# Where the operands of a matmul lie: down products, gate and up rows, and the load of the constants

## The chip, the cores and the metric

One Trainium2 chip, one core. The metric is the device time of one launch of the whole kernel, in microseconds. The kernel before takes 5654.88 us (median of three runs, 5647.37 to 5656.9).

## The reference

Two transformer blocks on 1024 tokens of width 1024, all in float32. The first holds an RWKV branch and a sparse attention branch. The second has two layers: latent attention beside a gated linear recurrence, then a SwiGLU feed-forward, dense in layer 0 and routed to 2 of 8 experts in layer 1. The parts that matter here:

```python
def _swiglu(h, w_gate, w_up, w_down):
    return (jax.nn.silu(h @ w_gate) * (h @ w_up)) @ w_down
...
    xs = xf[tok_sorted]
    hid = jax.nn.silu(lax.ragged_dot(xs, w_gate, group_sizes)) * lax.ragged_dot(xs, w_up, group_sizes)
    ys = lax.ragged_dot(hid, w_down, group_sizes)
```

The dense feed-forward is 1024 x 2816 x 1024, each expert's 1024 x 3584 x 1024.

## The kernel before

The program is a row of stages. Each has its own block of instructions for the five engines and ends in a barrier of all of them. `first_block` runs first. Its first stage, `norm_in` (`norm_transpose`), loads the eight row blocks of x, norms them (ScalarE squares, VectorE scales) and transposes them on TensorE, with the identity matrix `eye`, the first 128 columns of the constants `cst`. Ahead of it stands a stage of its own, `load_constants`, in which SyncE loads `cst` (128 x 3808) and `vec` (128 x 107) and waits for both.

The feed-forwards are `swiglu_passes` (dense, tiles named `dense_*`) and `expert_passes` (tiles named `experts_*`). Every float32 product is made of three matmuls of type float32r: each operand is split into a rounded part `high` and a rest `low`, and high x high, high x low and low x high are summed in PSUM. Both run over chunks of 128 hidden units; a chunk's weights are one load of 1.5 MB (`raw`: gate, up, down, each 128 x 1024), which ScalarE rounds to `high` and VectorE subtracts to `low`.

- Gate and up products: the stationary operand is a 128 x 128 block k of the weights, the moving operand is block k of the transposed rows `xs_high` or `xs_low` (`dense_xs_parts` in the dense block), 256 or 288 columns wide. Three matmuls for each k, 8 blocks, two products: 48 matmuls for each chunk.
- Down products: the stationary operand is 128 columns of the hidden values, `hid_high` or `hid_low`, the moving operand is a half, 512 columns, of the chunk's down weights. 12 matmuls for each chunk at 256 slots, 16 at 288.

The experts run 8 passes of 28 chunks, four of 288 slots and four of 256 as the trace's counts say (112 chunks of each width); the dense block runs 4 passes of 22 chunks with 256 rows.

```python
last = nc.tensor.matmul(ps[:, m, 0:width], w[:, u, m, c], x[:, k, 0:width], ...)        # gate, up: L3237
last = nc.tensor.matmul(ps[:, 2 + 2 * a + h, :], x, w[:, v, 2, c], ...)                 # down: L3229
```

(The second argument is the stationary operand, the third the moving one. In the rows of a profile the moving operand is named first.) Weights are prepared two chunks ahead: ScalarE and VectorE work on chunk n+2 while TensorE works on chunk n, and SyncE asks for a load when `split` says that the buffer `raw` is free.

Tiles lie in SBUF one behind the other, in the order in which the stage names them (`st.sb`). A tile's address here is its byte offset in each partition, and its *rest* is that address modulo 512. Blocks of 128 float32 columns are 512 bytes, so all 128-column blocks of a tile whose rows are whole multiples of 512 bytes have the tile's rest. `xs_high` of the experts has rows of 288 columns, 1152 bytes, so that its block k lies 128 k bytes further modulo 512. The float32r products of the other stages (`proj`, L2099; `out_proj`, L1725 to L1727) have both operands at the same rest, 448.

Of the kernel before, what the change touches and what calls it, by code (L numbers as in the profile page):

```python
# [8 lines left out]
F32R = mybir.dt.float32r  # L9
# [8 lines left out]
P = 128  # L18
NT = T // P
KD = D // P  # L20
# [122 lines left out]

def load_constants(core):
    nc, d = core.nc, core.dram
    st = Stage(core, "const")
    loaded = st.sem("loaded")
    with nc.Block("const") as block:
        @block.sync
        def _(sp):  # L150
            sp.dma_start(core.cst[:, :], d["constants"]).then_inc(loaded, 16)
            sp.dma_start(core.vec[:, :], d["vectors"]).then_inc(loaded, 16)
            sp.wait_ge(loaded, 32)
    st.end()


def norm_transpose(core, name, x, xT, gain, source, out=None, room=None, router=None, moves=()):

# [5 lines left out]
    U = 4 if router is None else 3  # L164
    router_in, beside = st.sem("router_in"), st.sem("beside")
    parts = xT if isinstance(xT, tuple) else None
# [10 lines left out]
    with nc.Block(name) as block:  # L177
        @block.sync
        def _(sp):
            if router is not None:  # L180
                sp.dma_start(router[:, :, :], core.dram["router"]).then_inc(router_in, 16)
            for b in range(NT):
                sp.dma_start(x[:, b, :], source[b * P:(b + 1) * P, :]).then_inc(loaded[b], 16)
                if b == 0:
                    sp.dma_start(row[:, :], core.dram[gain].to_broadcast([P, D])).then_inc(gain_in, 16)
            for to, origin in moves:
                sp.dma_start(to, origin).then_inc(beside, 16)
# [70 lines left out]
        def _(pe):  # L258
            def score(b):
# [3 lines left out]
                for k in range(KD):  # L263
                    nc.tensor.matmul(core.ps[:, 6, b * NEXP:(b + 1) * NEXP], xT[:, k, b * P:(b + 1) * P], router[:, k, :],
                                     start=(k == 0), stop=(k == KD - 1))

            for b in range(NT):
                pe.wait_ge(scaled, b + 1)
                if b >= U:
                    pe.wait_ge(rounded, b - U + 1)  # L270
                    if parts:
                        pe.wait_ge(placed, b - U + 1)
                for k in range(KD):
                    last = nc.tensor.transpose(ps4[:, b % U, k, :], xs[:, b % R, k * P:(k + 1) * P], core.c("eye"))
                last.then_inc(turned, 1)
                if router is not None and b:
                    score(b - 1)
# [2452 lines left out]
def swiglu_passes(core, name, NC, weights, out, experts=None, tiles=None, residual=None):  # L2730
# [19 lines left out]
    high = st.sb("high", [P, NB, 3, D], F32R)  # L2750
    low = st.sb("low", [P, NB, 3, D], F32R)
    index = st.sb("index", [P, 2], U32)
    xs = st.sb("xs", [P, 2, D])
# [4 lines left out]
    hid = st.sb("hid", [P, 2, SLOTS])  # L2758
    hid_high = st.sb("hid_high", [P, 2, SLOTS], F32R)
    hid_low = st.sb("hid_low", [P, 2, SLOTS], F32R)  # L2760
    y = st.sb("y", [P, 2, D])
# [311 lines left out]
def expert_passes(core, name, NC, weights, out, experts, tiles, slots, index):  # L3073
# [17 lines left out]
    high = st.sb("high", [P, NB, 3, D], F32R)  # L3091
    low = st.sb("low", [P, NB, 3, D], F32R)
    token = st.sb("token", [P, NT], U32)
    xs = st.sb("xs", [P, 3, D])
    xs_high = st.sb("xs_high", [P, KD, ROOM], F32R)
    xs_low = st.sb("xs_low", [P, KD, ROOM], F32R)
    silu = st.sb("silu", [P, 2, ROOM])
    hid = st.sb("hid", [P, 2, ROOM])


    hid_high = st.sb("hid_high", [P, 2, KEPT], F32R)
    hid_low = st.sb("hid_low", [P, 2, MAIN], F32R)
    y = st.sb("y", [P, 3, D])
# [385 lines left out]
def build(nc, dram, dump=None, until=None):  # L3489

    with ExitStack() as ctx:
        core = Core(nc, dram, ctx)
        load_constants(core)
        first_block(core, dump)
# [84 lines left out]
def first_block(core, dump):  # L3579
    nc, d = core.nc, core.dram  # L3580
    with nc.sbuf_tensor("big", [P, 5, 4, T], F32) as big:
        flat = big[:, :, :, :].rearrange("p a j n -> p (a j) n")
        with nc.sbuf_tensor("masks", [P, offset(NT) - offset(TOPK // P)], F32) as masks, nc.sbuf_tensor("small", [P, T], F32) as small:
            down, queries, relu = flat[:, 0:4, :], flat[:, 8:10, :], flat[:, 10:12, :]
            with nc.sbuf_tensor("index_weight", [P, NT, IDX_HEADS], F32) as weight, ExitStack() as s2:
                xT = split_tensors(core, s2, "xT", [P, KD, T])
                norm_transpose(core, "norm_in", as_rows(flat[:, 0:8, :]), xT, "norm_row", d["x"])
                projections(core, "proj", d["w_in"], xT, [(4, ACT.Copy, lambda n: at(down, n), None),
# [202 lines left out]
```

## Time and profile before

| what | value |
|---|---|
| median of 3 runs | 5654.88 us |
| the profiled execution | 5654.06 us, span of its instructions 5652.3 us |
| granted TensorE clock, mean | 0.954 |
| TensorE busy | 92% of the span |
| VectorE, ScalarE busy | 49%, 39% |
| experts (gate, up, down) | 3415.6 to 5581 us |
| dense block | 1860 to 2611 us |

The duration that a row gives for a matmul includes its way through the array, which overlaps with the next matmul. The rate is read from the starts: the distance of two starts divided by the number of matmuls between them.

### The profile page before, as it was taken

How to read it: one execution, taken by the hardware profiler on the slowest of the kernel's cores; microseconds unless marked ns; L12 is line 12 of the kernel's file. 1: busy time of each engine (PE TensorE's matmuls, PEld its weight loads, DVE VectorE, ACT ScalarE, POOL GpSimd, SP SyncE). 2: the span in 40 equal slices, each digit the busy share in tenths (PEclk: the TensorE clock that was granted, in tenths of full speed). 3: DMA queues.
4: the chain of work that ended last, by engine and by line, in shares of the span. 5: the costliest groups of instructions: out<-in, count | busy, mean ns of one | idle time of the engine just before them, and what ended most of it. 6: DMA issues, size and time to landing. Idle time of an engine off the chain costs nothing. (4 is left out here: it accounts for less than half of the span.)

```text
span 5652.3 us, 97257 instructions
## 1 busy us (share of the span) xinstructions
PE 5191.5 (92%) x38308; PEld 4533.0 (80%) x38309; DVE 2744.8 (49%) x4394; ACT 2225.0 (39%) x3437; POOL 345.9 (6%) x564
## 2 busy tenths in 40 slices
PE   6896989899899899997989988999999999999994
PEld 5574977677677899996877677989898999999994
DVE  2497545333844455554156444444444555555444
ACT  2353236232443444443234423333334444444432
POOL 0121100000600000000023001000000000000001
PEclk8996999999999999998999998999999999999997
DMA  1110010311003655553100424444444554555544
GB/s 68 49 64 22 0 36 1 120 59 34 3 17 120 238 211 203 190 205 115 45 16 19 137 112 174 155 162 155 159 154 170 187 188 179 204 187 188 184 156 187
DMA packets 104464, 688.49 MB, mean 122 GB/s; under 512 B 12304, under 2 KB 16160, under 8 KB 63136
## 3 DMA queue, kind: packets, MB, share of 16 engines
q1 hardware_dynamic: 90608, 639.74, 31.4%
q0 software_dynamic: 8816, 27.44, 1.3%
q10 hardware_dynamic: 4800, 17.83, 0.8%
q8 instruction: 186, 3.05, 0.2%
q14 instruction: 54, 0.44, 0.0%
HBM read 622.67 MB, written 62.29 MB: 121 GB/s over the span
## 5 line engine op out<-in xcount | busy, mean ns | idle before, releaser
L3373 DVE TENSOR_TENSOR experts_low<-experts_raw,experts_high 128x1024 fp32r<-128x1024 f32 x678 | 810.8, 1224 | 1005.9 <-ACT experts_high L3302 1005.9
L3237 PE MATMUL ps<-experts_xs_high,experts_high 128*128 128x256 f32 (+1 forms) x3584 | 1038.4, 290 | 38.0 <-issue 36.1
L3237 PE MATMUL ps<-experts_xs_high,experts_low 128*128 128x256 f32 (+1 forms) x3584 | 1039.2, 290 | 2.0 <-issue 1.9
L3237 PE MATMUL ps<-experts_xs_low,experts_high 128*128 128x256 f32 (+1 forms) x3584 | 1037.8, 290 | 0.0
L3237 PEld LDWEIGHTS ps<-experts_xs_high,experts_high 128*128 128x128 f32 x3584 | 681.4, 190 | 53.2 <-issue 43.7
L3302 ACT ACTIVATE experts_high<-experts_raw 128x1024 fp32r<-128x1024 f32 x678 | 687.9, 1049 | 30.7 <-DMA experts_raw<-experts 30.7
L3237 PEld LDWEIGHTS ps<-experts_xs_low,experts_high 128*128 128x128 f32 x3584 | 680.0, 190 | 9.7 <-issue 0.5
L3237 PEld LDWEIGHTS ps<-experts_xs_high,experts_low 128*128 128x128 f32 x3584 | 680.8, 190 | 0.4 <-issue 0.4
L2912 PE MATMUL ps<-dense_xs_parts,dense_high 128*128 128x256 f32 x2816 | 498.5, 280 | 4.0 <-DVE dense_xs_parts L3015 2.7
L2912 PEld LDWEIGHTS ps<-dense_xs_parts,dense_high 128*128 128x128 f32 x2816 | 436.2, 188 | 12.3 <-issue 4.7
L3229 PE MATMUL ps<-experts_high,experts_hid_high 128*128 128x512 f32 x1120 | 444.7, 397 | 0.0
L3229 PE MATMUL ps<-experts_low,experts_hid_high 128*128 128x512 f32 x1120 | 441.8, 394 | 0.0
L3326 ACT ACTIVATE experts_silu<-ps 128x288 f32<-128x288 f32 (+1 forms) x224 | 89.1, 398 | 817.6 <-PE ps L3237 811.4
L2912 PE MATMUL ps<-dense_xs_parts,dense_low 128*128 128x256 f32 x1408 | 393.4, 279 | 0.0
L3021 DVE TENSOR_TENSOR dense_low<-dense_raw,dense_high 128x1024 fp32r<-128x1024 f32 x270 | 323.2, 1222 | 66.5 <-ACT dense_high L2950 66.5
L3229 PE MATMUL ps<-experts_high,experts_hid_low 128*128 128x512 f32 x896 | 354.2, 395 | 0.0
L2950 ACT ACTIVATE dense_high<-dense_raw 128x1024 fp32r<-128x1024 f32 x270 | 283.8, 1054 | 48.7 <-PE ps L2897 22.4
L2912 PEld LDWEIGHTS ps<-dense_xs_parts,dense_low 128*128 128x128 f32 x1408 | 265.3, 188 | 0.0
L3332 ACT ACTIVATE experts_hid_high<-experts_hid 128x288 fp32r<-128x288 f32 (+1 forms) x224 | 96.6, 431 | 411.0 <-DVE experts_hid L3391 411.0
L3229 PEld LDWEIGHTS ps<-experts_low,experts_hid_high 128*128 128x128 f32 x1120 | 210.5, 188 | 39.9
L3229 PEld LDWEIGHTS ps<-experts_high,experts_hid_high 128*128 128x128 f32 x1120 | 210.5, 188 | 39.8
L3229 PEld LDWEIGHTS ps<-experts_high,experts_hid_low 128*128 128x128 f32 x896 | 168.3, 188 | 40.8
(538 smaller groups left out, 9118.3 us busy)
## 6 DMA issues: line engine op xcount, KB each, us to landing
experts_raw<-experts SPq DMA_DIRECT2D x226, 1536.0 KB
dense_raw<-dense SPq DMA_DIRECT2D x90, 1536.0 KB, 6.2
mixT<-w_in SPq DMA_DIRECT2D x36, 512.0 KB
y_slot<-mla_blank SPq DMA_DIRECT2D x15, 1152.0 KB
out_proj_raw<-w_out SPq DMA_DIRECT2D x48, 256.0 KB, 2.8
proj_keys_raw<-w_in SPq DMA_DIRECT2D x20, 512.0 KB
x_mixed<-mixT SPq DMA_DIRECT2D x16, 512.0 KB, 2.6
h_rows<-out_proj_rows SPq DMA_DIRECT2D x16, 512.0 KB
```

Source lines behind the costliest of these rows:

```text
L2912: last = nc.tensor.matmul(bank(u, m, SLOTS), w[:, u, m, c], x[:, k, :], start=(k == 0 and i == 0), stop=(k == KD - 1 and i == 2))
L2950: nc.scalar.activation(high[:, v, t, :], raw[:, v, t, :], ACT.Copy).then_inc(rounded, 1)
L3021: nc.vector.tensor_tensor(low[:, v, t, :], raw[:, v, t, :], high[:, v, t, :].bitcast(F32), ALU.subtract).then_inc(split, 1)
L3229: last = nc.tensor.matmul(ps[:, 2 + 2 * a + h, :], x, w[:, v, 2, c], start=first and i == 0, stop=last_one and i == len(terms) - 1)
L3237: last = nc.tensor.matmul(ps[:, m, 0:width], w[:, u, m, c], x[:, k, 0:width], start=(k == 0 and i == 0), stop=(k == KD - 1 and i == 2))
L3302: nc.scalar.activation(high[:, v, t, :], raw[:, v % NR, t, :], ACT.Copy).then_inc(rounded, 1)
L3326: nc.scalar.activation(silu[:, u % 2, 0:width], ps[:, 0, 0:width], ACT.Silu).then_inc(silu_done, 1)
L3332: nc.scalar.activation(hid_high[:, u % 2, 0:width], hid[:, u % 2, 0:width], ACT.Copy).then_inc(hid_rounded, 1)
L3373: nc.vector.tensor_tensor(low[:, v, t, :], raw[:, v % NR, t, :], high[:, v, t, :].bitcast(F32), ALU.subtract).then_inc(split, 1)
```

## The change

1. `load_constants` goes. `norm_in` loads `eye` behind the first row block and the gain, and the rest of `cst` and `vec` behind the last row block (its argument `moves`); TensorE waits for `eye_in` before its first transpose, and SyncE waits for the rest at the end of the stage.
2. In both feed-forwards `hid_high` and `hid_low` are placed right behind `low`.
3. In the experts the rows of `xs_high` and `xs_low` become KEPT = 384 columns (1536 bytes) instead of ROOM = 288. The matmuls read the same 256 or 288 of them.

```diff
-def load_constants(core):
-    nc, d = core.nc, core.dram
-    st = Stage(core, "const")
-    loaded = st.sem("loaded")
-    with nc.Block("const") as block:
-        @block.sync
-        def _(sp):
-            sp.dma_start(core.cst[:, :], d["constants"]).then_inc(loaded, 16)
-            sp.dma_start(core.vec[:, :], d["vectors"]).then_inc(loaded, 16)
-            sp.wait_ge(loaded, 32)
-    st.end()
...
                 if b == 0:
                     sp.dma_start(row[:, :], core.dram[gain].to_broadcast([P, D])).then_inc(gain_in, 16)
+                    if eye is not None:
+                        sp.dma_start(core.c("eye"), eye).then_inc(eye_in, 16)
             for to, origin in moves:
                 sp.dma_start(to, origin).then_inc(beside, 16)
...
+            if eye is not None:
+                pe.wait_ge(eye_in, 16)
             for b in range(NT):
                 pe.wait_ge(scaled, b + 1)
...
@@ swiglu_passes
     low = st.sb("low", [P, NB, 3, D], F32R)
+    hid_high = st.sb("hid_high", [P, 2, SLOTS], F32R)
+    hid_low = st.sb("hid_low", [P, 2, SLOTS], F32R)
     index = st.sb("index", [P, 2], U32)
...
-    hid_high = st.sb("hid_high", [P, 2, SLOTS], F32R)
-    hid_low = st.sb("hid_low", [P, 2, SLOTS], F32R)
...
@@ expert_passes
     low = st.sb("low", [P, NB, 3, D], F32R)
+    hid_high = st.sb("hid_high", [P, 2, KEPT], F32R)
+    hid_low = st.sb("hid_low", [P, 2, MAIN], F32R)
     token = st.sb("token", [P, NT], U32)
+    xs_high = st.sb("xs_high", [P, KD, KEPT], F32R)
+    xs_low = st.sb("xs_low", [P, KD, KEPT], F32R)
     xs = st.sb("xs", [P, 3, D])
-    xs_high = st.sb("xs_high", [P, KD, ROOM], F32R)
-    xs_low = st.sb("xs_low", [P, KD, ROOM], F32R)
     silu = st.sb("silu", [P, 2, ROOM])
     hid = st.sb("hid", [P, 2, ROOM])
-    hid_high = st.sb("hid_high", [P, 2, KEPT], F32R)
-    hid_low = st.sb("hid_low", [P, 2, MAIN], F32R)
...
-        load_constants(core)
...
-                norm_transpose(core, "norm_in", as_rows(flat[:, 0:8, :]), xT, "norm_row", d["x"])
+                norm_transpose(core, "norm_in", as_rows(flat[:, 0:8, :]), xT, "norm_row", d["x"], eye=d["constants"][:, 0:P],
+                               moves=[(core.vec[:, :], d["vectors"]), (core.cst[:, P:NCST], d["constants"][:, P:NCST])])
```

The addresses that follow, as the two built programs have them (moving less stationary is the difference of the two rests, modulo 512):

| products | stationary, rest | moving, rest | moving less stationary before | after |
|---|---|---|---|---|
| dense down | `hid_*` 480, after 448 | `high`, `low` 448 | 480 (32 below) | 0 |
| experts down | `hid_*` 256, after 224 | `high`, `low` 224 | 480 (32 below) | 0 |
| dense gate, up | `high`, `low` 448 | `xs_parts` 480 | 32 | 32 |
| experts gate, up | `high`, `low` 224 | `xs_*` 256 + 128 k, after 256 | 32, 160, 288, 416 by turns of k | 32 |
| `proj`, `out_proj` | 448 | 448 | 0 | 0 |

The order of the instructions changes in two places only. The first is SyncE's queue, from the program's start to the first load of the stage `proj`; `const_loaded` and `norm_in_beside` are what it waits for. Before:

```order
L3777 ISA
L149 UNCONDITIONAL_BRANCH [waits barrier_Pool_Activation_PE_DVE_SP_release]
L151 DMA cst<-constants 128x3808
L152 DMA vec<-vectors 128x107
L148 UNCONDITIONAL_BRANCH [waits const_loaded]
L178 UNCONDITIONAL_BRANCH [waits barrier_Pool_Activation_PE_DVE_SP_release]
L183 DMA big<-x 128x1024
L185 DMA norm_in_gain<-norm_row 128x1024
L183 DMA big<-x 128x1024 x7
L177 UNCONDITIONAL_BRANCH
L364 UNCONDITIONAL_BRANCH [waits barrier_Pool_Activation_PE_DVE_SP_release]
```

And after, in the same place (`big` is the space that x is loaded into):

```order
L3766 ISA
L165 UNCONDITIONAL_BRANCH [waits barrier_Pool_Activation_PE_DVE_SP_release]
L170 DMA big<-x 128x1024
L172 DMA norm_in_gain<-norm_row 128x1024
L174 DMA cst<-constants 128x128
L170 DMA big<-x 128x1024 x7
L176 DMA vec<-vectors 128x107
L176 DMA cst<-constants 128x3680
L164 UNCONDITIONAL_BRANCH [waits norm_in_beside]
L355 UNCONDITIONAL_BRANCH [waits barrier_Pool_Activation_PE_DVE_SP_release]
```

One stage with its wait and its barrier is gone, the identity (64 KB) stands between the gain and the second row block, and the other constants stand behind the eighth. The second place is TensorE's first instructions, the transposes of the norm stage, after the change:

```order
L3766 ISA
L246 UNCONDITIONAL_BRANCH [waits barrier_Pool_Activation_PE_DVE_SP_release]
L265 MATMUL ps<-cst,norm_in_scaled 128x128 [waits norm_in_scaled,norm_in_eye_in]
L265 MATMUL ps<-cst,norm_in_scaled 128x128 x7
L265 MATMUL ps<-cst,norm_in_scaled 128x128 [waits norm_in_scaled]
```

Before, the third of these rows waited for `norm_in_scaled` alone; now the first transpose waits for `eye_in` too; nothing else has moved on TensorE, VectorE or ScalarE, and no matmul is added, removed or reshaped.

## Rows read from the trace of the kernel before

**Rows 1.** Waits of TensorE, 3430 to 5640 us: who for whom, us, times, longest.

```profile
...
PE ps L3237 <- issue: 35.9, 10, 10.1
...
```

**Rows 2.** Groups of TensorE by shape: stationary and moving sizes, count, busy us, mean ns.

```profile
...
L3237 PE MATMUL ps<-experts_xs_high,experts_low 128*128 128x288 f32 x1792 | 534.0, 298 | 2.0 <-issue 1.9
...
L3237 PE MATMUL ps<-experts_xs_high,experts_low 128*128 128x256 f32 x1792 | 505.2, 282 | 0.0
...
L3229 PE MATMUL ps<-experts_high,experts_hid_high 128*128 128x512 f32 x1120 | 444.7, 397 | 0.0
...
L3229 PE MATMUL ps<-experts_high,experts_hid_low 128*128 128x512 f32 x896 | 354.2, 395 | 0.0
...
L2897 PE MATMUL ps<-dense_high,dense_hid_high 128*128 128x512 f32 x352 | 139.7, 397 | 1.0 <-DVE dense_hid_low L3046 1.0
...
```

**Rows 3.** Timeline of TensorE, one chunk of the experts, 288 slots: start, duration.

```profile
...
3805.72 0.39 PE L3229 MATMUL ps<-experts_high,experts_hid_high 128*128 128x512 f32 x1
...
3809.44 0.30 PE L3237 MATMUL ps<-experts_xs_high,experts_high 128*128 128x288 f32 x1
...
3809.84 0.30 PE L3237 MATMUL ps<-experts_xs_high,experts_high 128*128 128x288 f32 x1
...
3810.25 0.29 PE L3237 MATMUL ps<-experts_xs_high,experts_high 128*128 128x288 f32 x1
...
3810.64 0.30 PE L3237 MATMUL ps<-experts_xs_high,experts_high 128*128 128x288 f32 x1
...
3815.85 0.39 PE L3229 MATMUL ps<-experts_high,experts_hid_high 128*128 128x512 f32 x1
...
```

**Rows 4.** Timeline of TensorE, one chunk of the experts, 256 slots.

```profile
...
4880.06 0.28 PE L3237 MATMUL ps<-experts_xs_high,experts_high 128*128 128x256 f32 x1
...
4885.71 0.40 PE L3229 MATMUL ps<-experts_high,experts_hid_high 128*128 128x512 f32 x1
...
4888.51 0.28 PE L3237 MATMUL ps<-experts_xs_high,experts_high 128*128 128x256 f32 x1
...
```

**Rows 5.** Timeline of TensorE, one chunk of the dense block.

```profile
...
2101.95 0.39 PE L2897 MATMUL ps<-dense_high,dense_hid_high 128*128 128x512 f32 x1
...
2104.75 0.40 PE L2912 MATMUL ps<-dense_xs_parts,dense_high 128*128 128x256 f32 x2
...
2110.35 0.39 PE L2897 MATMUL ps<-dense_high,dense_hid_high 128*128 128x512 f32 x1
...
```

**Rows 6.** Timeline of TensorE, input projection (L2099), 90 matmuls apart.

```profile
...
1300.27 0.61 PE L2099 MATMUL ps<-xT_high,proj_high 128*128 128x512 f32 x2
...
1320.67 0.61 PE L2099 MATMUL ps<-xT_high,proj_high 128*128 128x512 f32 x2
...
```

**Rows 7.** Timeline of TensorE, output projection (L1725), 45 matmuls apart.

```profile
...
1029.70 0.39 PE L1725 MATMUL ps<-out_proj_high,out_proj_x_high 128*128 128x512 f32 x1
...
1039.90 0.39 PE L1725 MATMUL ps<-out_proj_high,out_proj_x_high 128*128 128x512 f32 x1
```

**Rows 8.** Timeline of all engines, 0 to 45 us: the first two stages.

```profile
...
0.90 0.41 SPq L151 DMA_DIRECT2D cst<-constants  x1
...
9.60 0.33 SPq L183 DMA_DIRECT2D big<-x  x1
...
16.63 1.06 ACT L203 ACTIVATE norm_in_junk<-big 128x1024 f32<-128x1024 f32 x1 [2.26 <-DMA big<-x]
...
20.87 4.18 PE L274 MATMUL ps<-cst,norm_in_scaled 128*128 128x128 f32 x24 [20.87 <-DVE norm_in_scaled L239]
...
36.74 4.61 DVE L245 TENSOR_TENSOR xT_low<-ps,xT_high 128x1024 fp32r<-128x1024 f32 x4
...
```

**Rows 9.** Windows: TensorE, loads, VectorE, ScalarE, GpSimd busy; granted clock, DMA share, GB/s.

```profile
...
10.50:24.00 13.50, 3.13 (x16) 3.14 (x17) 4.59 (x10) 7.57 (x15) 0.00 (x0) 1.00 0.92 350
24.00:41.00 17.00, 8.26 (x50) 6.52 (x48) 15.86 (x22) 11.22 (x20) 0.00 (x0) 0.79 0.00 0
4560.00:4800.00 240.00, 238.94 (x1694) 223.34 (x1693) 123.42 (x145) 105.43 (x147) 2.41 (x3) 0.99 0.53 190
...
```

More of the change, by code:

```diff
@@ L141, in pairs, with norm_transpose @@
         body(count - 1, 0, count // 2)
-def load_constants(core):
-    nc, d = core.nc, core.dram
-    st = Stage(core, "const")
-    loaded = st.sem("loaded")
-    with nc.Block("const") as block:
-        @block.sync
-        def _(sp):
-            sp.dma_start(core.cst[:, :], d["constants"]).then_inc(loaded, 16)
-            sp.dma_start(core.vec[:, :], d["vectors"]).then_inc(loaded, 16)
-            sp.wait_ge(loaded, 32)
-    st.end()
-def norm_transpose(core, name, x, xT, gain, source, out=None, room=None, router=None, moves=()):
+def norm_transpose(core, name, x, xT, gain, source, out=None, room=None, router=None, moves=(), eye=None):
     nc = core.nc
@@ L164, in norm_transpose @@
     U = 4 if router is None else 3
-    router_in, beside = st.sem("router_in"), st.sem("beside")
+    router_in, beside, eye_in = st.sem("router_in"), st.sem("beside"), st.sem("eye_in")
     parts = xT if isinstance(xT, tuple) else None
```

## The prediction

> **What bounds the kernel now.** I read the page first: TensorE is busy for 92% of the span, VectorE for half, so the question is TensorE's own rate wherever nothing is late for it. Next the waits of TensorE in the expert stage: 35.9 us in all are left to nothing but issue [rows 1], of some 2150 us; no other engine and no load keeps it waiting for long. In one window of that stage TensorE is busy for 238.94 of 240 us, VectorE for 123.42, ScalarE for 105.43, the DMA engines for 0.53 of the time, at a granted clock of 0.99, that is nearly always 2.4 GHz [rows 9]. So a matmul there that follows its predecessor sooner shortens the span by as much, and the other engines have room for it.
>
> The rates come from the starts in the timeline. At 2.4 GHz one column a cycle would be 213.3 ns for 512 columns, 120.0 for 288, 106.7 for 256. What the rows show:
> - Input projection: 90 matmuls of 512 columns in 1320.67 - 1300.27 = 20.40 us, 226.7 ns each [rows 6]. Output projection, weights moving and activations stationary as in a down product: 45 in 10.20 us, 226.7 ns too [rows 7].
> - Down products: 16 in 3809.44 - 3805.72 = 3.72 us, 232.5 ns [rows 3]; 12 in 4888.51 - 4885.71 = 2.80 us, 233.3 ns [rows 4]; in the dense block 12 in 2104.75 - 2101.95 = 2.80 us, 233.3 ns [rows 5].
> - Gate and up: 48 of 288 columns in 3815.85 - 3809.44 = 6.41 us, 133.5 ns [rows 3]; 48 of 256 in 4885.71 - 4880.06 = 5.65 us, 117.7 ns [rows 4]; in the dense block 48 of 256 in 2110.35 - 2104.75 = 5.60 us, 116.7 ns [rows 5].
>
> So the same shape at the same clock takes 226.7 ns in two stages and 233 in two others. What goes with it is the table of rests: the first pair has moving and stationary operand at one rest, the second pair 32 bytes apart. The experts' gate and up rows, whose distance changes with k, take 1.0 ns more than the dense block's, which are always 32 apart.
>
> **The change part by part.**
>
> *The constants' stage.* SyncE asks for `cst` at 0.90 and for the first block of x at 9.60 [rows 8]; with the stage gone that request stands first, and all behind it comes 8.7 us sooner. Against that: `eye`, 64 KB, is put ahead of the second block, whose landing starts ScalarE at 16.63 [rows 8]. Its issue is one more of 0.41 us like that of `cst` [rows 8], its 64 KB at the 350 GB/s of the x loads [rows 9] are 0.2 us. I take 0.4 us; the ends are 0 (both hidden behind the gain's transfer) and 1.5 (a first load that starts cold, and small packets). The wait for `eye` costs nothing: it is asked for before the second block, while the first transpose starts at 20.87 [rows 8], over 4 us after that block is there. The other constants are 1.93 MB; at 350 GB/s that is 5.5 us, and they stand behind the x loads. In 24 to 41 us, until the last of VectorE's `xT_low` that begin at 36.74 [rows 8], the queue moves nothing, a gap of 17 us [rows 9]. They lie under it; only at a third of that rate would SyncE's wait hold the barrier and `proj` behind it. Gain: 8.7 - 0.4 = **8.3 us**, from 7.2 to 8.7.
>
> *Down products at one rest.* 112 chunks of each width give 112 x 16 = 1792 and 112 x 12 = 1344 matmuls, together the 3136 of the groups (two groups of 1120 and one of 896); the dense block has three groups of 352, 1056 [rows 2]. With 226.7 ns each: 1792 x 5.8 = 10.4 us, 1344 x 6.6 = 8.9, 1056 x 6.6 = 7.0, together **26.3 us**. Ends: 0 if the distance isn't the cause (a rival, below), 28 if all pay 6.6 ns or a little more.
>
> A rule of the Trainium skill speaks against this step. "SBUF — State Buffer", section "Who interferes with whom", gives TensorE two independent read ports, one for the moving operand and one for the weight load, and says that PE never waits on anyone. By it the distance of the two operands can't matter, and this term would be 0. The trace doesn't agree: 226.7 against 233.3 ns for one shape is a difference that the rule has no place for, so I go by the rows.
>
> *Gate and up rows of the experts always 32 off.* At 256 columns the dense block shows the new state: 116.7 against 117.7 ns, 1.0 x 5376 = **5.4 us** (three groups of 1792) [rows 2]. At 288 columns no row shows it. The same share of a longer matmul is 1.1 ns, 1.1 x 5376 = **6.0 us**. For the bounds, the chunk itself: block k=1 (distance 160) lasts 3810.25 - 3809.84 = 0.41 us, block k=2 (288) 3810.64 - 3810.25 = 0.39 [rows 3]. If all 16 blocks took 0.39, the 48 would take 6.24 us, 0.17 less, 19 us over 112 chunks; if the two values differ by rounding alone, nothing. My 6.0 is nearer to the small end, where the 256-wide rows point. Block k=0, at distance 32, takes 3809.84 - 3809.44 = 0.40 [rows 3], the middle, which is why I don't go higher.
>
> *What becomes late next.* A 256-wide chunk takes 4888.51 - 4880.06 = 8.45 us now and would take 48 x 116.7 + 12 x 226.7 = 8.32. VectorE's share goes from 0.514 to 0.522, the DMA's from 0.53 to 0.54 [rows 9]: nothing turns up. The placement moves no weight tile, and the reads and writes of VectorE and ScalarE keep their shapes; I cost their new addresses at nothing, since they have half their time free.
>
> *Sum.* 8.3 + 26.3 + 5.4 + 6.0 = 46.0 us, from the profiled execution's 5654.06 to **5608 us**; the median of the runs is 0.8 us above that execution, which makes no odds.
>
> **The rivals.**
> 1. *The distance is not the cause; only the front comes in.* The 6.6 ns would belong to the feed-forward stages (their loops, their heavy loads). For it: these stages are also the ones with 190 GB/s of loads [rows 9]. Against it: the experts and the dense block differ in code, widths and rests and show the same 233.3 ns, and the 256-wide products differ by distance too. Time: 5654 - 8.3 = 5646. By the skill's two ports, this is what should happen.
> 2. *Down products as forecast, the 288-wide rows no faster or a little slower* (distance 32 repeated might be a bad pace for a row of 288). Gain 8.3 + 26.3 + 5.4 = 40.0, less up to 10 us if each block took the 0.41 of the slow ones ((0.41 x 16 - 6.41) x 112 = 17, of which half): 5614 to 5624.
> 3. *288-wide rows gain like k=2 does*: 19 in place of 6.0, 5595.
> 4. *Slower.* The stall goes by the moving operand's own rest, and a stride of 1536 puts all eight blocks of `xs_*` on one, 256, where four took turns. If that is the bad one, every 288-wide block lasts 0.41 us: 17 us more; the same share at 256 columns is 15 more; the down products' moving rest doesn't change, so they gain nothing. 5654 - 8.3 + 32 = 5678. It decides once the two widths together lose 20 us. Against it: the dense block has all its rows on one rest and is the fastest, and `out_proj` and the dense down products move from the same rest, 448, at 226.7 and 233.3 ns.
>
> **How the numbers follow.** My forecast 0.76, rival 1 0.07, rival 2 0.08, rival 3 0.05, rival 4 0.04. A measurement of this kernel tells 0.2%, 11 us, from no change. Faster by more: forecast, rivals 2 and 3, 0.89. Within: rival 1, whose 8.3 us is 0.15%, 0.07. Slower: 0.04. The range takes rivals 2 and 3 and leaves out 1 and 4: down to 5594, up to 5627.
>
> **What would show each step.** First load of x at about 0.9 us, and `proj`'s first matmul some 8.3 us sooner than before; a load still running when VectorE has written its last `xT_low` would show the barrier held. 12 down products in 2.72 us (16 in 3.63) instead of 2.80 (3.72): right; unchanged: rival 1. 48 gate and up matmuls in 5.60 us at 256 and 6.36 at 288, with all blocks of k alike: right; 6.56 at 288: rival 4. The prediction is wrong if the down products stay at 233 ns, or if the waits of TensorE grow in the expert stage.

## The result and the profile after

The changed kernel takes 5611.44 us (median of four runs, 5607.94 to 5619.1), the kernel before, beside it on the same chip, 5651.12 us (four runs, 5645.3 to 5656.9). The ratio is 0.9928, with a 95% interval of 0.9916 to 0.9939: 41 us faster, and well over the 0.2% that can be told from no change. The profiled execution took 5610.46 us, with a granted clock of 0.955 where it was 0.954. Line numbers in the experts are 11 lower than before (gate and up L3226, down L3218), in the dense block 9 lower (L2903, L2888).

The page of the kernel after, its span and its first part, busy time of the engines:

```profile
span 5608.8 us, 97235 instructions
...
PE 5165.1 (92%) x38308; PEld 4529.4 (81%) x38309; DVE 2740.6 (49%) x4394; ACT 2225.0 (40%) x3437; POOL 343.5 (6%) x564
```

The shares say nothing of a change. The waits of TensorE from 3420 to 5600 us, which answer to [rows 1]:

```profile
PE ps L3226 <- issue: 31.0, 9, 7.9
```

Nor has a wait gone: 31.0 us are left to issue, where there were 35.9. Most of the time came out of the pace of the matmuls, that is the distance of their starts. The timeline of TensorE in the kernel after, one chunk of the experts of 288 slots (down products, gate and up products, the next down products), the answer to [rows 3]:

```profile
3800.21 0.39 PE L3218 MATMUL ps<-experts_high,experts_hid_high 128*128 128x512 f32 x1
...
3803.84 0.30 PE L3226 MATMUL ps<-experts_xs_high,experts_high 128*128 128x288 f32 x1
...
3810.24 0.39 PE L3218 MATMUL ps<-experts_high,experts_hid_high 128*128 128x512 f32 x1
```

16 down products take 3.63 us and were 3.72; 48 gate and up products take 6.40 us and were 6.41. A chunk of 256 slots, the answer to [rows 4]; the second row shown is the sixth of its twelve down products:

```profile
4875.43 0.39 PE L3218 MATMUL ps<-experts_high,experts_hid_high 128*128 128x512 f32 x1
...
4876.58 0.39 PE L3218 MATMUL ps<-experts_high,experts_hid_low 128*128 128x512 f32 x1
...
4878.17 0.28 PE L3226 MATMUL ps<-experts_xs_high,experts_high 128*128 128x256 f32 x1
...
4883.77 0.39 PE L3218 MATMUL ps<-experts_high,experts_hid_high 128*128 128x512 f32 x1
```

Twelve down products take 2.74 us and were 2.80, 48 gate and up products 5.60 and were 5.65. The down products aren't alike: the first five take 4876.58 - 4875.43 = 1.15 us, 230 ns each or a little more, the seven behind them 4878.17 - 4876.58 = 1.59 us, 227 ns each. The dense block, the answer to [rows 5], is the same again, with 2.74 us in place of 2.80 from its first down product to the next gate product:

```profile
2101.07 0.39 PE L2888 MATMUL ps<-dense_high,dense_hid_high 128*128 128x512 f32 x1
...
2103.81 0.40 PE L2903 MATMUL ps<-dense_xs_parts,dense_high 128*128 128x256 f32 x2
```

And the start of the program, timeline of all engines, the answer to [rows 8]:

```profile
0.91 0.40 SPq L170 DMA_DIRECT2D big<-x  x1
1.36 0.42 SPq L172 DMA_DIRECT2D norm_in_gain<-norm_row  x1
1.83 0.42 SPq L174 DMA_DIRECT2D cst<-constants  x1
...
6.68 0.44 SPq L176 DMA_DIRECT2D cst<-constants  x1
...
8.41 1.06 ACT L192 ACTIVATE norm_in_junk<-big 128x1024 f32<-128x1024 f32 x1 [2.71 <-DMA big<-x]
...
12.73 4.70 PE L265 MATMUL ps<-cst,norm_in_scaled 128*128 128x128 f32 x24 [12.73 <-DVE norm_in_scaled L228]
...
28.57 4.61 DVE L234 TENSOR_TENSOR xT_low<-ps,xT_high 128x1024 fp32r<-128x1024 f32 x4
...
40.18 1.19 PE L378 MATMUL ps<-xT_high,proj_high 128*128 128x512 f32 x2 [9.64 <-DVE proj_low L421]
```

ScalarE's second square starts 8.22 us sooner, the transposes 8.14, the last `xT_low` 8.17, the first matmul of `proj` 8.1 (it was at 48.3 us). The transposes wait for VectorE, not for `eye`. The windows of the kernel after (columns as in [rows 9]) show that the other constants lie under this stage, and that nothing else turns up in the experts:

```profile
16.00:33.00 17.00, 9.38 (x50) 7.61 (x48) 16.02 (x22) 11.17 (x20) 0.00 (x0) 0.80 0.19 82
4525.00:4755.00 230.00, 228.31 (x1634) 215.56 (x1635) 117.22 (x135) 99.76 (x137) 2.83 (x3) 0.99 0.53 195
```

VectorE's share is 117.22 / 230 = 0.510 there, before it was 0.514.

From the start times of all matmuls of the feed-forward stages, at 2.4 GHz and with longer gaps (over 0.26 us behind a down product, 0.2 us behind the others) left out, the mean distance of two starts comes out as follows. The last column is the difference times the number of matmuls.

| products | count | before, ns | after, ns | gain, us |
|---|---|---|---|---|
| down, dense | 1056 | 233.32 | 228.75 | 4.8 |
| down, experts | 3136 | 232.98 | 227.65 | 16.7 |
| gate and up, experts, 256 columns | 5376 | 117.89 | 116.75 | 6.1 |
| gate and up, experts, 288 columns | 5376 | 133.41 | 133.35 | 0.3 |
| gate and up, dense | 4224 | 116.68 | 116.74 | -0.3 |

These make 27.6 us, with 8.1 us of the front 35.7. The two profiled executions are 43.6 apart. The two stages, each from its first product to its last, are 34.6 us shorter (2916.3 before, 2881.6 after). So 7.0 us of that lie between products (stalls, and stretches at the lower clock), and under 1 us is spread over the rest of the program.

### The profile page after: what moved, and what is told of

It is laid out like the page before. It is cut to its first block and busy times, and to the rows that moved or that the text cites. A ratio compares the mean times of both kernels' runs of the same rounds, so it can differ in the third digit from the quotient of the medians.

```text
span 5608.8 us, 97235 instructions
## 1 busy us (share of the span) xinstructions
PE 5165.1 (92%) x38308; PEld 4529.4 (81%) x38309; DVE 2740.6 (49%) x4394; ACT 2225.0 (40%) x3437; POOL 343.5 (6%) x564
## 5 line engine op out<-in xcount | busy, mean ns | idle before, releaser
L3226 PE MATMUL ps<-experts_xs_high,experts_high 128*128 128x256 f32 (+1 forms) x3584 | 1035.4, 289 | 30.3 <-issue 28.8
L3226 PE MATMUL ps<-experts_xs_high,experts_low 128*128 128x256 f32 (+1 forms) x3584 | 1033.8, 288 | 2.3 <-issue 2.3
L3226 PE MATMUL ps<-experts_xs_low,experts_high 128*128 128x256 f32 (+1 forms) x3584 | 1034.2, 289 | 0.0
L3226 PEld LDWEIGHTS ps<-experts_xs_high,experts_high 128*128 128x128 f32 x3584 | 678.8, 189 | 44.0 <-issue 35.8
L3226 PEld LDWEIGHTS ps<-experts_xs_low,experts_high 128*128 128x128 f32 x3584 | 678.9, 189 | 8.1
L3226 PEld LDWEIGHTS ps<-experts_xs_high,experts_low 128*128 128x128 f32 x3584 | 678.8, 189 | 0.0
L2903 PE MATMUL ps<-dense_xs_parts,dense_high 128*128 128x256 f32 x2816 | 499.3, 280 | 4.1 <-DVE dense_xs_parts L3006 2.7
L2903 PEld LDWEIGHTS ps<-dense_xs_parts,dense_high 128*128 128x128 f32 x2816 | 436.7, 189 | 11.3 <-issue 4.9
L3218 PE MATMUL ps<-experts_high,experts_hid_high 128*128 128x512 f32 x1120 | 438.5, 391 | 0.0
L3218 PE MATMUL ps<-experts_low,experts_hid_high 128*128 128x512 f32 x1120 | 437.1, 390 | 0.0
L2903 PE MATMUL ps<-dense_xs_parts,dense_low 128*128 128x256 f32 x1408 | 393.5, 279 | 0.0
L3218 PE MATMUL ps<-experts_high,experts_hid_low 128*128 128x512 f32 x896 | 348.8, 389 | 0.0
L2903 PEld LDWEIGHTS ps<-dense_xs_parts,dense_low 128*128 128x128 f32 x1408 | 265.7, 189 | 0.0
L3218 PEld LDWEIGHTS ps<-experts_high,experts_hid_high 128*128 128x128 f32 x1120 | 210.4, 188 | 36.0
L3218 PEld LDWEIGHTS ps<-experts_low,experts_hid_high 128*128 128x128 f32 x1120 | 210.2, 188 | 34.8
L3218 PEld LDWEIGHTS ps<-experts_high,experts_hid_low 128*128 128x128 f32 x896 | 168.2, 188 | 36.2
```

What stands on the lines that cost most here:

```text
L2903: last = nc.tensor.matmul(bank(u, m, SLOTS), w[:, u, m, c], x[:, k, :], start=(k == 0 and i == 0), stop=(k == KD - 1 and i == 2))
```

## Experiments: the three parts, each alone

The theory is that of the prediction: the pace goes by the distance of the two operands. Its rivals are that the stage sets it (rival 1), that a moving operand's own rest does (rival 4), and that the gain in time isn't the sum of such paces at all.

Each kernel is the one before with a single part of the change. The three shared the runs of the kernel before (20, median 5651.89 us).

**Part 1, the front.**

```diff
-        load_constants(core)
...
+                norm_transpose(core, "norm_in", as_rows(flat[:, 0:8, :]), xT, "norm_row", d["x"], eye=d["constants"][:, 0:P],
+                               moves=[(core.vec[:, :], d["vectors"]), (core.cst[:, P:NCST], d["constants"][:, P:NCST])])
```

> The change's first part alone: no stage for the constants, all tiles where they were. Both theories (the distance of the two operands sets the matmul's pace; or the pace belongs to the stage): the first matmul of the input projection 8.1 us sooner, as in the changed kernel, and 8 us off the time, near 5643 us, ratio 0.9986. Down products stay at 233 ns. What it tells apart: the changed kernel's waits of TensorE at the passes' starts in the expert stage were 5 to 10 us shorter. If that comes from where the code lies, it shows here too, in the same places; if it is chance, it doesn't, or elsewhere.

**Part 2, the place of the hidden values, in both stages.**

```diff
     low = st.sb("low", [P, NB, 3, D], F32R)
+    hid_high = st.sb("hid_high", [P, 2, KEPT], F32R)
+    hid_low = st.sb("hid_low", [P, 2, MAIN], F32R)
```

> The hidden values' tiles alone are moved (dense and experts) to the rest of the weights; stage of the constants and 1152-byte rows as before. Distance theory: down products 233 to 228 ns in the experts, 234 to 229 in the dense block, 4.9 x 3136 + 4.5 x 1056 = 20 us, 5631 us, ratio 0.9964. Rival (the pace belongs to the feed-forward stages): nothing, 5651 us. A rival inside the first theory: the first five down products of a 256-wide chunk, slow in the changed kernel, are slow because gate and up rows keep a fixed distance of 32 before them; then in the expert stage, where the distances still change with k here, they are not slow in the same way, while the dense block's are.

**Part 3, the stride of the rows.**

```diff
-    xs_high = st.sb("xs_high", [P, KD, ROOM], F32R)
-    xs_low = st.sb("xs_low", [P, KD, ROOM], F32R)
+    xs_high = st.sb("xs_high", [P, KD, KEPT], F32R)
+    xs_low = st.sb("xs_low", [P, KD, KEPT], F32R)
```

> The experts' gate and up rows alone get the stride of 1536 bytes (distance 32 for every k); the hidden values stay 32 bytes off the weights. Distance theory, as the changed kernel's trace has it: 256 columns 117.85 to 116.7 ns (5.9 us), 288 columns unchanged at 133.3 ns; 5645 us, ratio 0.999. My prediction's own figure, 132.4 ns at 288 columns, would give 5 us more, 5640 us. Theory of the moving operand's own rest: also a change at 288 columns, one way or the other, by more than 1 ns.

| kernel | median, us (runs) | ratio, 95% interval | gain, us, and its interval |
|---|---|---|---|
| front alone | 5640.54 (10) | 0.9979, 0.9969 to 0.9988 | 12 (7 to 18) |
| down alone | 5630.54 (5) | 0.9965, 0.9951 to 0.9980 | 20 (11 to 28) |
| rows alone | 5641.63 (10) | 0.9985, 0.9976 to 0.9995 | 8 (3 to 14) |

The three gains sum up to 40 us, the change's own is 41: within these intervals the parts add. Part 1 and part 2 came out at their expected times, 5643 and 5631 us. For part 3 the two expected times, 5645 and 5640, lie too near to each other for the runs; the trace decides. The timeline of the kernel with part 2 alone, a chunk of 288 slots and one of 256:

```profile
3803.09 0.39 PE L3227 MATMUL ps<-experts_high,experts_hid_high 128*128 128x512 f32 x1
...
3806.74 0.30 PE L3235 MATMUL ps<-experts_xs_high,experts_high 128*128 128x288 f32 x1
...
4867.70 0.28 PE L3235 MATMUL ps<-experts_xs_high,experts_high 128*128 128x256 f32 x1
...
4873.35 0.40 PE L3227 MATMUL ps<-experts_high,experts_hid_high 128*128 128x512 f32 x1
...
4876.11 0.28 PE L3235 MATMUL ps<-experts_xs_high,experts_high 128*128 128x256 f32 x1
```

Down products 3.65 us for 16 and 2.76 for 12, gate and up still 5.65 for 48. The expectation's inner rival is borne out: with the rows' distance still changing with k, eight of the experts' twelve down products behind a 256-wide half are slow (233, 236, 224, 231, 236, 228, 232, 231 ns in the mean of 104 chunks) and three of sixteen behind a 288-wide one, while the dense block has its five (230, 236, 228, 232, 231). With part 3 alone, the same view:

```profile
3807.10 0.40 PE L3227 MATMUL ps<-experts_high,experts_hid_high 128*128 128x512 f32 x1
...
3810.83 0.30 PE L3235 MATMUL ps<-experts_xs_high,experts_high 128*128 128x288 f32 x1
...
3817.23 0.40 PE L3227 MATMUL ps<-experts_high,experts_hid_high 128*128 128x512 f32 x1
...
4869.59 0.28 PE L3235 MATMUL ps<-experts_xs_high,experts_high 128*128 128x256 f32 x1
...
4875.19 0.39 PE L3227 MATMUL ps<-experts_high,experts_hid_high 128*128 128x512 f32 x1
```

Down products back at 3.73 us, gate and up 5.60 at 256 columns, and 6.40 at 288: nothing gained there. The parts aren't quite apart, though. The experts' down products take 228.7 ns with part 2 alone and 227.65 in the changed kernel: the steady rows before them give another 3.3 us, which the runs are too coarse to show.

The stalls tell why more can't be read out of single profiles. What TensorE's waits leave to issue in the experts is 37.1 us in the kernel with part 1 alone, 33.4 with part 2, 35.0 with part 3. The shorter waits of the changed kernel, several us at the passes' starts, follow no part of the change; only one profile of each kernel was taken, so their cause stays open.

## Experiments: the distance by itself

**A map of distances.** Matmuls alone, with no other engine at work; the reference's computation is left out in this kernel and in the three below that are called "matmuls alone". The operands lie in one buffer at chosen addresses, and the products come in the kernel's order.

```python
high, low, xh, xl = o, 1024 + o, 4096 + o + s, 4096 + 8 * 384 + o + s      # s: distance, o: shift of both
for k in range(8):
    for i, (w, v) in enumerate(((high, xh), (high, xl), (low, xh))):
        nc.tensor.matmul(ps[:, m, 0:width], flat[:, w + k * P:w + (k + 1) * P], flat[:, v + k * stride:v + k * stride + width], ...)
```

> A kernel of matmuls alone, on float32r copies of x, without the reference's computation: runs of 24 matmuls of 512 columns (down products' order), 48 of 256 and 48 of 288 (gate and up order) at each of 21 distances from 0 to 496 bytes, one after the other with no wait between; then the same at distances 0 and 32 with both operands shifted by 32, 64, 128 and 256 bytes; then stationary blocks that take turns between two rests; then whole chunks, gate and up followed by down products, at several pairs of distances. Distance theory: at 512 columns 226.7 ns at 0 and 233 at 480 and at 32, the same whatever shifts both; somewhere among the 21 a distance better than 32 for 256 and 288 columns (116.7 and 133.3 ns). Own-rest theory: the time changes when both are shifted, and not with the distance. Ports theory (two independent read ports): one time for each width at every distance. The slow start of the down products behind a 256-wide chunk comes back in the chunks (32, 0) and should be gone where both distances are 0, if it is the changeover that costs.

Timeline of TensorE in this kernel. First the distances 32 and 64, each with 24 products of 512 columns, then 48 of 256 and 48 of 288 (one group in the rows); then both operands shifted by 32 bytes, at distance 0 and at distance 32, 24 products of 512:

```profile
126.65 5.76 PE L72 MATMUL ps<-buf 128*128 128x512 f32 x24
132.24 12.16 PE L62 MATMUL ps<-buf 128*128 128x256 f32 x96
...
161.88 5.67 PE L72 MATMUL ps<-buf 128*128 128x512 f32 x24
167.39 11.92 PE L62 MATMUL ps<-buf 128*128 128x256 f32 x96
...
425.74 5.62 PE L72 MATMUL ps<-buf 128*128 128x512 f32 x24
431.20 3.04 PE L62 MATMUL ps<-buf 128*128 128x256 f32 x24
...
434.08 5.76 PE L72 MATMUL ps<-buf 128*128 128x512 f32 x24
439.68 1.56 PE L62 MATMUL ps<-buf 128*128 128x256 f32 x12
```

24 products of 512 columns take 132.24 - 126.65 = 5.59 us at distance 32 and 5.51 at 64. With both operands 32 bytes further they take 5.46 us at distance 0 and 5.60 at distance 32, as without the shift. Shifts of 64, 128 and 256 bytes gave the same pairs (226.6 to 226.9 and 233.3 to 233.4 ns, the first few products left out). So at these two distances an operand's own address doesn't count, the difference does. The paces in the last half of each run, ns for one matmul:

| distance, bytes | 512 columns | 256 | 288 |
|---|---|---|---|
| 0 | 226.7 | 120.0 | 131.7 |
| 4 | 237.5 | 123.3 | 135.5 |
| 16 | 231.7 | 116.7 | 131.7 |
| 32 | 233.3 | 116.7 | 133.3 |
| 64 | 228.9 | 113.3 | 131.7 |
| 128 | 233.3 | 118.8 | 133.3 |
| 160 | 234.3 | 118.8 | 133.3 |
| 192 | 233.3 | 113.3 | 133.3 |
| 256 | 226.7 | 120.0 | 131.7 |
| 288 | 233.3 | 116.7 | 133.3 |
| 320 | 228.9 | 117.8 | 132.2 |
| 416 | 234.6 | 117.3 | 133.3 |
| 480 (before, down) | 233.3 | 118.3 | 133.3 |

For the distances 0 and 32 it repeats after 256 bytes, and the best distance differs with the width. Distances 0 and 256 are the fastest for 512 columns and poor ones for 256. For 288 columns the four distances that the rows had by turns, 32, 160, 288 and 416, all give 133.3, which is why the new stride gained nothing there; for 256 columns 32 has the best pace of the four. The chunks at the end of the map also show the five slow down products: behind 48 products of 256 columns at distance 32 the twelve take 230, 236, 228, 233, 231 ns and then 226 or 227; behind products of 288 columns at distance 32 all take 225 to 227. With gate, up and down all at distance 0 this slow head is there too, so it isn't the change of distance that makes it.

One more part of the map lets the stationary blocks take turns between two places, 32 bytes apart. With distances 32 and 0 by turns the pace is 233.3 ns, that of 32 alone; with 0 and 480 by turns it is 235.0 (232, 236, 232, 240), slower than 0 or 480 alone.

**Two paces at one distance.** By the map, 64 is better than 32 for both widths. More matmuls alone, with the map's code and other strides and pairs: `PAIRS` are the distances of `xs_high` and `xs_low` with the stride in columns, `CHUNKS` the distances of gate and up, of down, and the columns, four chunks each:

```python
PAIRS = [(d, d, 384) for d in (32, 64, 192, 320, 448, 56, 72, 80)] + ...
CHUNKS = [(g, e, width) for width, gs in ((256, (32, 64, 192, 448)), (288, (32, 0, 64, 96, 256))) for g in gs for e in (0, 64)]
```

> The second map, matmuls alone again (the reference's computation is left out). First runs of 96 gate and up matmuls at 256 and at 288 columns, with the distances of xs_high and xs_low chosen apart, and a step of 1536 or 1152 bytes between blocks k. Then four chunks in a row of gate and up at distance g and down products at distance e, for g of 32, 64, 192, 448 (256 columns) and 32, 0, 64, 96, 256 (288 columns), e of 0 and 64. Distance theory with a period of 256 bytes: 113.3 ns at 64, 192, 320 and 448 for 256 columns once the run has settled; for 288 columns, whose rows end half a period further, the rest that matters moves by 128 with every matmul, so that the step of 1152 with xs_low 128 bytes further than xs_high should do better than 131.7 ns, down to 127.5 (17/16 of 120, as 226.7 and 113.3 are 17/16 of 213.3 and 106.7); if the distance modulo 512 at the start is all that counts, that step does no better than the others. Chunks: the slow start of the down products depends on g and width; with g = 64 it may be shorter or longer than with 32, which the first map leaves open.

Its timeline, the pair (64, 0) with its first and second chunk, and the second chunk of (64, 64):

```profile
699.38 5.60 PE L62 MATMUL ps<-buf 128*128 128x256 f32 x48
704.82 2.91 PE L71 MATMUL ps<-buf 128*128 128x512 f32 x12
707.57 5.82 PE L62 MATMUL ps<-buf 128*128 128x256 f32 x48
713.22 2.92 PE L71 MATMUL ps<-buf 128*128 128x512 f32 x12
...
741.22 5.60 PE L62 MATMUL ps<-buf 128*128 128x256 f32 x48
746.66 2.91 PE L71 MATMUL ps<-buf 128*128 128x512 f32 x12
```

The same 48 matmuls, at the same addresses and clock, take 5.44 us (113.3 ns) in one chunk and 5.65 (117.85) in the next. There are two paces at distance 64, and what ran ahead decides which. The long runs show the same: 64, 192 and 320 bytes, for which I had expected 113.3 ns, settled at 117.8 in this kernel and only 448 at 113.3, while in the first map 64 and 192 had 113.3. No stride or distance brought 288 columns below 131.1 ns; the 127.5 that I had hoped for wasn't found.

**Distance 64 in the kernel.** The whole change, and with it the experts' and the dense block's rows 32 bytes further (tiles ahead of them are made larger, and no more of them is used than before):

```diff
-    index = st.sb("index", [P, 2], U32)
+    index = st.sb("index", [P, 16], U32)
...
-    token = st.sb("token", [P, NT], U32)
+    token = st.sb("token", [P, 2 * NT], U32)
```

> The changed kernel with the gate and up rows 64 bytes off the weights' rest in both feed-forwards, where it had 32; nothing else differs. Distance theory by the first map: 256 columns 116.7 to 113.3 ns, 3.4 x (5376 + 4224) = 32.6 us; 288 columns 133.3 to 131.7, 1.6 x 5376 = 8.6 us; less what the down products' start loses, at most 2 us for each 100 chunks and 20 ns: 5611 - 41 = 5570 us, ratio to the kernel before 0.9855. Rival (what the map shows of matmuls alone is lost in the kernel, since ScalarE, VectorE and loads use SBUF beside them): 5611 us. Rival (the chunk is then limited by another engine): TensorE starts to wait, in between.

The same with the down products at 64 too, in both stages. The lines are those of the experts; the dense block gets the same gap, and its `index` has 32 columns:

```diff
+    st.sb("gap", [P, 112])
     hid_high = st.sb("hid_high", [P, 2, KEPT], F32R)
     hid_low = st.sb("hid_low", [P, 2, MAIN], F32R)
-    token = st.sb("token", [P, NT], U32)
+    token = st.sb("token", [P, 4 * NT], U32)
```

> The changed kernel with distance 64 for gate and up and for the down products, in both feed-forwards. In the second map 64 had two paces at 256 columns, 113.3 and 117.8 ns, and which one a run took hung on what stood before it: with down products at 0 it fell to 117.8 and stayed there, with down products at 64 it was at 113.3 from the second chunk on, whole chunk 8187 ns, where (32, 0), the changed kernel's pair, has 8347. Theory of the carried state (a run's pace is set by its distances and by the state in which the run before leaves the operand reads): 256 columns 113.3 ns, down products 228.9, 0.16 us less for each of the 200 chunks of 256 columns, 32 us; 288 columns 131.7 in place of 133.3, down products 228.7 in place of 226.9, 0.05 x 112 = 5 us less: 5611 - 37 = 5574 us, ratio to the kernel before 0.986. Rival (the kernel's own waits and loop ends reset the state, so that the slower pace comes back): 117.8 ns, near 5618 us as with 64 and 0.

The kernel with gate and up at 64 took 5617.74 us (five runs), ratio 0.9937 (0.9924 to 0.9951). The one with the down products at 64 too took 5617.69 us, 0.9932 (0.9918 to 0.9946). Both expectations fell, by over 40 us: neither is faster than the changed kernel. What came is the second expectation's rival, the slower pace and 5618 us. The second one's timeline, a chunk of 256 slots:

```profile
4871.44 0.39 PE L3220 MATMUL ps<-experts_high,experts_hid_high 128*128 128x512 f32 x1
...
4874.19 0.28 PE L3228 MATMUL ps<-experts_xs_high,experts_high 128*128 128x256 f32 x1
...
4879.85 0.40 PE L3220 MATMUL ps<-experts_high,experts_hid_high 128*128 128x512 f32 x1
```

5.66 us for 48, the slow pace; the mean over the whole stage is 117.8 in both. At 288 columns they did reach 131.8 and 132.0 ns, near the map's 131.7.

**What loses the quick pace.** First, whether a loop's end does: matmuls alone, each pair in a loop of six chunks.

> Matmuls alone (the reference's computation is left out): for each pair of distances, g for gate and up and e for the down products, both in steps of 32 from 0 to 224, a loop of 6 chunks without other waits, at 256 and at 288 columns. Carried-state theory: the time of a settled chunk depends on both distances together and not on the sum of two single terms; (32, 0) stands near 8350 and 10027 ns, (64, 64) near 8187 and 9980. It is to show whether any pair is clearly below both, and how rare the 113.3 ns pace is. If the loop's end resets the state, (64, 64) comes back with 117.8.

With (64, 64) all six chunks took 8.18 to 8.19 us, the quick pace; with (64, 0) the first took 8.18 and the others 8.41; with (32, 0), the changed kernel's pair, 8.35. So a loop's end does nothing, and the kernel with both at 64 should have been quick.

The grid has all pairs of eight distances each, and once settled no pair is quicker at 256 columns than (64, 64). It also shows that a product's own distance isn't the whole of it: gate and up at 32 settled at 116.7 ns with the down products at 0 and at 117.8 with them at 192, and of the sixteen pairs with gate and up at 64 or 192 only seven held 113.3 to 113.5 ns.

Then four things that a kernel has between its products:

```python
if how == "met":
    pe.wait_ge(made, 24)
if how == "stall":
    last.then_inc(asked, 1)
    pe.wait_ge(told, count[0])      # ScalarE answers with an activation of 8 columns
if how == "turn":
    for k in range(4):
        nc.tensor.matmul(ps[:, 6, k * P:(k + 1) * P], rows[:, 4, k * P:(k + 1) * P], rows[:, 5, 0:P], start=True, stop=True)
```

> Matmuls alone on TensorE, reference's computation left out. Chunks of 48 gate and up products of 256 columns and 12 down products; for the pair of distances (64, 64), then (32, 0): groups of four chunks, in turn with nothing between the products; with waits that are already met after gate, up and down; nothing; with real stalls there (ScalarE answers each); nothing; with four float32 transposes after gate and after up; nothing; with ScalarE and VectorE reading and writing SBUF beside them; nothing. Theory: at 64 the quick pace, 113.3 ns, is lost at a real stall or at a transpose and stays lost in the chunks behind it, 117.8, so that the kernel, which has both, never keeps it; at 32 all stays at 116.7. Rival 1: waits that are already met are enough to lose it. Rival 2: it is the SBUF traffic of the other engines, so only the last but one group is slow. Rival 3: nothing of this loses it, all groups at 113.3, and what the kernel does otherwise stays open.

Its timeline at (64, 64): an undisturbed chunk and the gate and up products of the first chunk with stalls; two undisturbed chunks after the four with stalls; gate and up products of a chunk with transposes; two undisturbed chunks after the four with transposes:

```profile
146.00 5.60 PE L89 MATMUL ps<-buf 128*128 128x256 f32 x48
151.44 2.91 PE L102 MATMUL ps<-buf 128*128 128x512 f32 x12
...
154.18 2.88 PE L89 MATMUL ps<-buf 128*128 128x256 f32 x24
157.36 3.10 PE L89 MATMUL ps<-buf 128*128 128x256 f32 x24 [0.30 <-ACT small L54]
...
211.34 5.82 PE L89 MATMUL ps<-buf 128*128 128x256 f32 x48
219.74 5.82 PE L89 MATMUL ps<-buf 128*128 128x256 f32 x48
...
238.34 2.88 PE L89 MATMUL ps<-buf 128*128 128x256 f32 x24
...
241.87 3.07 PE L89 MATMUL ps<-buf 128*128 128x256 f32 x24
...
268.62 5.60 PE L89 MATMUL ps<-buf 128*128 128x256 f32 x48
276.80 5.60 PE L89 MATMUL ps<-buf 128*128 128x256 f32 x48
```

Waits that are already met change nothing, nor do ScalarE and VectorE at work beside. A stall of 0.30 us turned the pace from 113.3 to 117.8, and it stayed so in the chunks behind it, for as long as nothing disturbed them (219.74 - 211.34 = 8.40 us a chunk, where it had been 154.18 - 146.00 = 8.18). The transposes did both: the up products right behind four of them ran at 117.8 (the row at 241.87), the gate products that came behind transposes and down products at 113.3 again (238.34), and the undisturbed chunks behind the four kept 113.3. At (32, 0) gate and up stayed at 116.6 to 117.0 ns from the second chunk on, stalls, transposes or not; there the stalls changed the down products, which had no slow head behind one. So my theory holds for the stall. For the transposes its first half holds, the quick pace is lost right behind them, and its second falls: it didn't stay lost.

**Experts at 64, the dense block at 32.** The last kernel takes for each stage what the runs made the cheaper.

```diff
@@ expert_passes, on top of the whole change
-    token = st.sb("token", [P, NT], U32)
+    token = st.sb("token", [P, 2 * NT], U32)
```

> The changed kernel with the experts' gate and up rows at distance 64 in place of 32; dense block and all down products as in the changed kernel. By the paces of the run with 64 in both stages (117.84 for 256 columns, 131.72 for 288): 5376 x 1.1 = 5.9 us lost, 5376 x 1.6 = 8.7 us gained, 5611.4 - 2.8 = about 5609, and 5 us better than the run with 64 in both. Rival: the head of slow down products behind a 256-wide half changes too, by up to 5 us either way. If the quick pace of 113.3 came in the experts, 5586.

5613.71 us (five runs), ratio 0.9932 (0.9918 to 0.9945). The paces came as expected, 117.8 and 131.7 ns in the experts and 116.7 in the dense block. The forecast gain of 3 us over the changed kernel is smaller than such a measurement can tell, and none is seen. The trace has a price that the forecast left to its rival: the experts' down products went from 227.65 to 228.9 ns, 4 us, which takes up the gain. None of these kernels is shown to beat the changed one.

## Why the prediction was right, step by step

*The front.* 8.3 us forecast, 8.1 to 8.2 in the trace at each of the four landmarks, 7 to 18 by the runs. The 0.4 us for `eye` was of the right size (2.30 - 1.83 = 0.47 us for its issue), and the constants' wait held nothing.

*Down products.* The mechanism was right: the distance of the two operands, and not the stage, sets the pace. The map shows it with no load and no other engine about, and part 2 alone shows it in the kernel. The size was off: 26.3 us forecast, 21.5 measured (4.8 + 16.7). At 288 slots the chunk gained a little more than forecast (3.73 to 3.63 us in the mean of 104 chunks, 6.3 ns for each product, where I took 5.8). At 256 slots and in the dense block I took the 226.7 ns of the projections, a long run of equal products; behind 48 products of 256 columns the first five are slow, and the mean is 228.7.

*Gate and up, 256 columns.* 5.4 us forecast, 6.1 measured, at the dense block's pace.

*Gate and up, 288 columns.* This step failed. "The same share of a longer matmul is 1.1 ns" had no ground: 6.0 us forecast, 0.3 measured. The pace depends on width and distance together, and the 0.39, 0.40 and 0.41 us of single blocks on which the bounds rested are the way in which one mean is spread: over 104 chunks the blocks of three took 397 and 403 ns by turns before and 399 and 401 after, at 133.4 ns a matmul both times. Rival 2 was right on this point, with its 40.0 us, which gives 5614; the up to 10 us that it set on a repeated distance of 32 did not come.

*The sum.* 46.0 us forecast, 43.6 between the profiled executions, 41 by the runs. The agreement of the first two is partly luck: the terms themselves make 35.7 us, about 10 less than forecast, and 7.0 us of shorter time between products, which no part explains and the forecast had at nothing, fill most of the gap. The runs' own 41 (34 to 47) holds both.

*The rivals.* Rival 1 falls: 226.7 against 233.3 ns in the map differ by distance alone. By the Trainium skill, "SBUF — State Buffer", section "Who interferes with whom", TensorE's read ports for the moving operand and for the weight load are independent, which leaves no room for that difference. The measurement decides against it for these float32r products. Rival 4 falls with the shifted operands. Rival 3 had the better pace at 288, and distance 32 doesn't have it: 131.7 ns exists at 0 and 64, and block k = 2 of the kernel before wasn't a sign of it.

What stays open: why the pace goes by the distance at all; whether it is the distance to a matmul's own stationary block or to the next one's, which is loaded beside it; where the head of five comes from; and which event of the kernel turns distance 64 to its slow pace. A stall of 0.30 us is enough, and the kernel has such stalls, but it also has transposes, behind which the pace was lost and came back, and I haven't tried them in the kernel's order.

## What to carry to other kernels

When TensorE is the bound and nothing is late for it, compare the distance of starts for one shape across stages; a difference at one clock can lie in where the two operands are placed to each other, and a reordered allocation is a cheap trial. Take the pace of a shape from a row with the same width and the same neighbours, since a share carried over from another width was worth nothing here, and a long run of equal products flattered the down products by 2 ns. A quick pace found in matmuls alone is not yet the kernel's: try it behind a stall first.

## What the runs showed of the hardware

- At 2.4 GHz the pace of float32r matmuls went by the difference of the two operands' addresses, the same at 0 and 256 bytes and at 32 and 288: 226.7 to 237.5 ns for 512 columns, 113.3 to 123.3 for 256, 131.1 to 135.5 for 288. One column a cycle would be 213.3, 106.7 and 120.0.
- The pace has a memory: 113.3 or 117.8 ns for the same matmuls at distance 64. A stall of 0.30 us turned it to 117.8 for the chunks behind. Right behind four float32 products of 128 columns it was 117.8, and behind such four and twelve down products 113.3 again. With gate and up at 32 and the down products at 0 it stayed at 116.6 to 117.0.
- Stationary blocks used by turns at distances 0 and 480 are slower than either alone: 232, 236, 232, 240 ns, mean 235.0, against 226.7 and 233.3. By turns at 32 and 0 they take 233.3, as at 32 alone.
